# Twice as many tokens with fetched first products in a two-layer decoder trunk, and narrower dense products

## The reference

```python
q = (xt @ w_q).reshape(T, 8, 2, 128)
s = einsum('thpc,hpnc->thpn', q, sub_keys)      # two scores per head over 128 keys
s1, i1 = top_k(s[:, :, 0], 16); s2, i2 = top_k(s[:, :, 1], 16)
# the 16 best of the 256 sums name 16 experts per head: expert = i1 * 128 + i2
gate = softmax(top_s)
h = gelu(einsum('cd,chkd->chk', xc, u[expert]))  # 8 x 16 = 128 first products per token
out = einsum('chk,chkd->cd', gate * h, v[expert])
```

## Time and profile before

| | us |
|---|---|
| median of 3 runs (lowest, highest) | 3177.66 (3174.99, 3183.06) |
| the profiled execution | 3181.07 |
| its span, first to last instruction | 3179.3 |
| TensorE busy | 3118.7 (98%) |
| VectorE busy | 2585.5 (81%) |
| ScalarE busy | 1632.1 (51%) |
| GpSimd busy | 1115.8 (35%) |
| moved by DMA | 846.06 MB, mean 266 GB/s |

### The profile page before, as it was taken

The page is one execution under the profiler, slowest core; times in us unless marked ns, Lnnn a source line. Parts: engine busy times, 40 slices in busy tenths (PEclk is TensorE's granted clock), DMA queues, the critical chain, the costliest instruction groups (busy, mean ns, idle before and its releaser), DMA issues.

```text
span 3179.3 us, 48912 instructions
## 1 busy us (share of the span) xinstructions
PE 3118.7 (98%) x17820; PEld 2787.0 (88%) x17820; DVE 2585.5 (81%) x5352; ACT 1632.1 (51%) x3079; POOL 1115.8 (35%) x658
## 2 busy tenths in 40 slices
PE   8999999999999999999999989999999999999999
PEld 7878899999998888888978868899999998888887
DVE  5686899999967888885378876899999967888885
ACT  5343249696943333335356654247696954333333
POOL 1002364656532445530000001365546532455540
PEclk9999999999999999999999999999999999999999
DMA  5113279898999999994222214269999999999994
GB/s 193 48 60 126 89 222 371 298 393 313 409 385 331 380 396 395 388 353 132 69 87 74 85 64 146 81 196 342 322 388 318 390 388 328 379 400 391 397 373 146
DMA packets 338079, 846.06 MB, mean 266 GB/s; under 512 B 28368, under 2 KB 161072, under 8 KB 336816
## 3 DMA queue, kind: packets, MB, share of 16 engines
q1 hardware_dynamic: 259504, 557.68, 49.4%
q0 software_dynamic: 78336, 285.25, 23.3%
HBM read 735.77 MB, written 107.05 MB: 265 GB/s over the span
## 4 chain that ended last, share of the span: by engine, by line
PE 38%; DVE 7%; ACT 2%; DMA 2%; issue 1%; SPq 0%; DVEq 0%; ACTq 0%
PE p_bank L2479 16%; PE p1r_h_ps L2405 11%; PE ba_bank L420 6%; PE o_bank L1763 1%; PE p1r_gate_ps L2463 1%; DMA gates<-x 1%; DVE p_grow L2906 1%; PE ba_oT_ps L482 1%; PE ba_t_ps L504 1%; DVE p1r_table L2796 1%; DVE p1r_table L2791 1%; PE p1r_s_ps L2429 0%; DMA gates<-p1r_gbuf 0%; DVE p1r_table L2786 0%; DVE p1r_table L2737 0%
## 5 line engine op out<-in xcount | busy, mean ns | idle before, releaser
L2548 ACT ACTIVATE peer_hi<-raw 128x1024 fp32r<-128x1024 f32 x540 | 571.3, 1058 | 668.3 <-PE p_bank L2479 618.2
L2891 DVE TENSOR_TENSOR peer_lo<-raw,peer_hi 128x1024 fp32r<-128x1024 f32 x434 | 531.1, 1225 | 265.4 <-ACT peer_hi L2548 260.4
L2361 POOL TENSOR_TENSOR peer_lo<-raw,peer_hi 128x1024 fp32r<-128x1024 f32 x106 | 274.1, 2586 | 1048.3 <-ACT peer_hi L2548 1047.1
L2379 POOL DMA_INDIRECT p_grow<-in_v_rows,p_expert x256 | 400.3, 1564 | 467.7 <-DVE p_acc L2915 375.9
L2379 POOL DMA_INDIRECT p_grow<-in_u_rows,p_expert x256 | 385.3, 1505 | 386.9 <-DVE p_hid L2906 338.3
L2479 PE MATMUL p_bank<-peer_hi,p_w_lo 128*128 128x512 f32 x1500 | 461.9, 389 | 0.0
L2479 PE MATMUL p_bank<-peer_hi,p_w_hi 128*128 128x512 f32 x1500 | 461.7, 389 | 0.0
L2479 PE MATMUL p_bank<-peer_lo,p_w_hi 128*128 128x512 f32 x1500 | 461.7, 389 | 0.0
L2405 PE MATMUL p1r_h_ps<-h_hi,peer_hi 128*128 128x368 f32 (+2 forms) x1152 | 394.0, 342 | 6.8 <-DVE peer_lo L2891 6.6
L2405 PE MATMUL p0r_h_ps<-h_hi,peer_hi 128*128 128x368 f32 (+2 forms) x1152 | 394.8, 343 | 5.5 <-DVE peer_lo L2891 5.4
L2405 PE MATMUL p0r_h_ps<-h_hi,peer_lo 128*128 128x368 f32 (+2 forms) x1152 | 388.8, 338 | 0.0
(11 more groups left out here) (481 smaller groups left out, 5626.7 us busy)
## 6 DMA issues: line engine op xcount, KB each, us to landing
raw<-in_u SPq DMA_DIRECT2D x256, 512.0 KB
raw<-in_v SPq DMA_DIRECT2D x256, 512.0 KB
p_g_sb<-gates SPq DMA_DIRECT2D x64, 768.0 KB
hiddens<-p_h_sb SPq DMA_DIRECT2D x240, 192.0 KB
p_w_raw<-hiddens SPq DMA_DIRECT2D x60, 768.0 KB
gates<-x SPq DMA_DIRECT2D x48, 512.0 KB
raw<-in_w_b_mix SPq DMA_DIRECT2D x38, 512.0 KB, 3.5
raw<-in_w_peer_q SPq DMA_DIRECT2D x32, 512.0 KB, 4.5
```

Of the source, the lines that this page charges most:

```text
L2361: pool.tensor_tensor(lo[:, m % NH, :], raw[:, m % NR, :], hi[:, m % NH, :].bitcast(F32), ALU.subtract).then_inc(lo_pool, 1)
L2379: pool.indirect_dma_start(out=grow[:, g % RG, :], out_offset=None, in_=table, in_offset=bass.IndirectOffsetOnAxis(ap=names[:, at:at + 1], ...
L2548: act.activation(hi[:, n % NH, :], raw[:, n % NR, :], ACT.Copy).then_inc(hi_ready, 1)
L2891: dve.tensor_tensor(lo[:, m % NH, :], raw[:, m % NR, :], hi[:, m % NH, :].bitcast(F32), ALU.subtract).then_inc(lo_dve, 1)
```

## The change

NE goes from 16 to 32, so SPREAD from 8 to 4 partitions per token and NJ from 16 to 32 gathers; FEW0 from 32 to 16, so the few rows come after 16 rows of tile 0 and not after 32. The dense products begin at column 160 and have 352 columns. `is_few` now holds for four batches of 8 tokens, not two. The rate of rows is 18 tenths instead of 16 per block before block 129. ROWS_ALL becomes 288; from the rates, the last few row comes at block 68, the turn of the weights at block 81, and SUM0 is 256. Three tensors in DRAM take the new shape. Nothing else changes: the blocks of the routing, of the placements and of the gate stores stand where they stood.

```diff
     PART = 32
-    NE = 16
+    NE = 32
     SPREAD = P // NE
     NJ = PAIRS // SPREAD
-    FEW0 = PART
+    FEW0 = PART // 2
     ROWS_ALL = 2 * PAIRS + NJ
@@ def row_tenths(n)
         if n < WEIGH0:
-            return 16
+            return 18
         return 7 if n < FRONT + 4 * CH else 13
@@ def trunk
-        few_x_dram = nc.dram_tensor("few_x", (16, P // 16, D), F32).ap()
-        few_dram = nc.dram_tensor("few", (16, 2, HEADS * TOPK), F32).ap()
-        few_w_dram = nc.dram_tensor("few_w", (P, HEADS * TOPK * 16 // P), F32).ap()
+        few_x_dram = nc.dram_tensor("few_x", (32, P // 32, D), F32).ap()
+        few_dram = nc.dram_tensor("few", (32, 2, HEADS * TOPK), F32).ap()
+        few_w_dram = nc.dram_tensor("few_w", (P, HEADS * TOPK * 32 // P), F32).ap()
```

## The result

The changed kernel takes 3201.76 us (median; 3199.36 to 3203.88), the kernel before on the same chip 3178.98 (3174.99 to 3183.06): a ratio of 1.0068 (95%: 1.0047 to 1.0090), slower by 23 us. The forecast was 3183, its range ended at 3200. The profiled execution has a span of 3202.1 us against 3179.3.

What follows compares the result with a forecast made beforehand. TensorE was taken to set the pace except at blocks 37, 64, 97 (waiting for VectorE) and 136 (last gate store). Per layer 0 + 0.5 - 1.0 + 3.3 = +2.8, for two +5.6: 3183 us, range 3159 to 3200.

Steps and rivals of the forecast that it cites:

- Blocks 16 to 36: Stretch before the first rendezvous: the 3.2 us saved become a longer wait for VectorE, 0 us, between 0 and +1.
- The rows' price on VectorE: Each fetched row costs VectorE 1.14 us; four more rows add 4.6 us in blocks 37 to 63 and in 64 to 96.
- the rendezvous: Blocks 37, 64 and 97, where TensorE waits for VectorE's routing; what lies between two is as long as VectorE needs.
- Blocks 37 to 63: Stretch of 125.8 us, forecast 126.3, that is +0.5 us per layer; ends -2.4 and +4.6.
- 64 to 96: Stretch of 154.7 us, forecast 153.7, that is -1.0 us per layer; ends -3.5 and +4.6.
- I keep 2.9 us of 7.0: In blocks 37 to 63, 2.9 of VectorE's 7.0 us idle time was taken to stay after four more rows.
- The second rival: Placements stall on gate stores once over about 2 us join 11.88: +8.3 us per layer, 3194 us; chance 0.20.
- Blocks 97 to 143: Stretch of 212.4 us, held by the last gate store ahead of block 136: +3.4 and +3.2 us, ends -6.5 and +6.
- The landing and the load behind it as before: Before block 136, the 14.00 us wait for the last gate store and the 7.54 us load were taken as unchanged.
- The clock's 1.7 us: At block 136, a lower clock after TensorE's wait was to add 5.67 - 4.00 = 1.7 us.
- The products: Dense products going from 368 to 352 columns were to save TensorE 0.16 us per block of 24.
- 352 columns cost as much as 368: Rival for the dense products: narrower ones save nothing, +2.3 us per layer more, 3188 us; chance 0.10 shared with another rival.

Runs made afterwards that it cites:

- both edits: Changed kernel with SyncE's first two gate loads three blocks later and each group's four gate-store parts issued in two blocks, not four: 3182.86 us, ratio 1.0013.
- Fewer bytes: Changed kernel with each u-block loaded over 820 of its 1024 columns, engines' work unchanged: 3182.71 us, ratio 1.0015.
- earlier stores: Changed kernel with the four parts of a gate store issued in two blocks instead of four: 3183.55 us, ratio 1.0014.
- the late gates' load: Changed kernel with SyncE's first two loads of gates three blocks later, at blocks 133 and 135: 3192.93 us, ratio 1.0037.

## Why the prediction was wrong

The forecast of 3183 us was 19 us short. A slower kernel had a chance of 0.33; what was given as a rival with a chance of 0.20, placements that stall on gate stores, happened. In blocks 37 to 96 it cost 11.7 us over the forecast, where the rival said 11; what goes beyond its 3194 us lies in blocks 97 to 143.

- **Blocks 16 to 36** (0 per layer, 0 to +1): -1.1 in both. Most of what the columns saved became a longer wait, as said.
- **The rows' price on VectorE**: right in size, 122.1 and 150.8 us of work. That it decides between the rendezvous failed in this kernel: VectorE was 93.6% busy in blocks 37 to 63, not over 96% (it was 96.5% in 64 to 96), and a product over 11% fewer numbers for each u row changed the time by nothing. With both edits VectorE is over 96% busy in all four stretches, and blocks 37 to 63 take 126.7 and 126.1 us, where the forecast had 126.3: there its picture may hold, which no run proves.
- **Blocks 37 to 63** (+0.5) were +1.8 and +4.7; **64 to 96** (-1.0) were +2.6 and +1.6. The step that failed is "I keep 2.9 us of 7.0", and 3.8 of 9.4. In layer 1 VectorE's idle time was 8.4 and 5.5 us, not 2.9 and 3.8, since a new wait came into it. The second rival has the mechanism: a store two blocks ahead of its use took 11.88 us and takes 15.19; the point it named, 2 us more, was passed. Fewer bytes (125.7 and 154.7 us in layer 0) and earlier stores (126.4 and 155.9) both shorten the stretches. A trace of the same code up to block 130, that of the late gates' load, has the two stretches together at +3.1 and +4.1 us over before, where this one has +4.4 and +6.3: the sign is sure, the size only to some 2 us.
- **Blocks 97 to 143** (+3.4 and +3.2) were +7.8 and +9.0, beyond their end of +6. The length up to the last store came out as forecast (+3.3 against +3.5 - 0.5), but by luck. The forecast had the queues move 45.3 MB at 416 GB/s; they moved 408 GB/s x 108.5 us = 44.3 MB, below the "over 410" it named, and the length came from TensorE's stalls in blocks 111 and 117. With the stores issued at two blocks, blocks 97 to 129 of layer 0 took 155.4 us under the same rows, where they took 157.5. "The landing and the load behind it as before" failed: the last store itself takes 4.0 us longer. The clock's 1.7 us measured 1.5 and 2.4 us (block 136 takes 5.53 and 6.39).
- **The products** (0.16 us a block): another term that failed, hidden here by the waits; it is why the columns gave nothing once the waits were gone. Blocks 17 to 35 run at 3.80 us (0.20 less); from block 38 on 352 columns take 4.00 nearly everywhere, also in blocks 127 to 134, which have no placement. Only behind a wait of TensorE does 3.80 come back (blocks 65 and 98). Two stretches of the timeline of PE in the changed kernel, ahead of the placements and among them; the distance of the first and last start over six products is 0.95 and 1.00 us:

```profile
2089.70 0.32 PE L2405 MATMUL p1r_h_ps<-h_hi,peer_hi 128*128 128x352 f32 x1
...
2090.65 0.32 PE L2405 MATMUL p1r_h_ps<-h_hi,peer_hi 128*128 128x352 f32 x1
...
2470.30 0.33 PE L2405 MATMUL p1r_h_ps<-h_hi,peer_hi 128*128 128x352 f32 x1
...
2471.30 0.33 PE L2405 MATMUL p1r_h_ps<-h_hi,peer_hi 128*128 128x352 f32 x1
```

  The rival that "352 columns cost as much as 368" was argued away with three widths; a fourth in between did not lie on their line. The Trainium skill (TensorE: Matmul & The Clock Gate, Back-to-back issue gap) gives 131 ns from one product of 512 columns to the next; no run here shows it, as 4.16 us for 24 products of only 384 columns is 173 ns each.
- **Sum.** Forecast +5.6, measured +25.0 in the counted blocks. Of the 19.4 us between, blocks 37 to 96 have 11.7 and 97 to 142 have 10; blocks 16 to 36 take 2.2 off. The span grew by 22.8; the 2.2 us gained outside these blocks were not followed.
- **What the text said would show it**: TensorE's idle time grew by 30.6 us (over 20), with waits of 4.1 and 5.2 us at block 136 in both layers (forecast 5 or more). Blocks near the forecast's 3.84 us (they took 3.80) stood ahead of block 36 and behind a few waits only. ScalarE waited 11 times for gate stores, named there as what would refute the forecast.

What stays open is why 352 columns have two paces, 158 and 167 ns a product, when 320 (147 ns), 368 (167) and 384 (173) have one each. The traces tell how they come. In the twelve kernels with 352 columns, both layers (24 cases), blocks 17 to 35 always ran at 3.80 us; block 38, behind the wait at 37 and ahead of the first placement, ran at 3.80 in 15 cases and at 4.00 in 9; and blocks 56 to 62, 89 to 95 and 127 to 131, behind placements, ran at 4.00 in all. It looks like a state that an interruption sets anew and that placements bring to the slower side; what the state is no run shows.

## What to carry to other kernels

When a change adds traffic to queues that are already full, look first for the operation that waits for a landing (a buffer that is free only when its store has landed, a load that stands behind another wait): two such landings took 28% and 29% longer here. Where the transfers are issued took 18 us off this kernel at no byte less, and 7 us off the kernel before. Then price the change with the same cure on both sides: 11.7 of its 23 us stayed. Before pricing a narrower product, ask how much of the time between two points where engines meet is TensorE's: here 13% fewer columns (320) gave 0.8% of the time.

## What the runs showed of the hardware

- One width of product, 352 columns, ran at two paces in one kernel: 3.80 and 4.00 us for 24, while its neighbours of 368 and 384 columns ran at 4.00 and 4.16, and 320 at 3.52, throughout. A cost per column read from widths on both sides need not hold for one between them.
- A store of 512 KB took 14.00 us in queues at 410 GB/s, and 18.01 us in queues at 408 GB/s in a kernel that asks for a tenth more rows there (39 instead of 35 in blocks 108 to 130). The added demand shows in the time of each transfer and not in GB/s. The 408 is no fixed ceiling: with the stores issued in another order the same kernel moved 416 over 104 us.
- After an idle time of TensorE of 5.2 us the granted clock was 0.50 for 3 us; after 3.6 us of waits in two pieces it had been 0.53. The blocks behind such waits, 97 and 136, took 1.7 to 2.9 us longer than the next one in the kernels before and after.
